# Hybrid attention, pooling and SwiGLU block on eight cores: last stores awaited behind the join, a hinted exit, a later table load and other vector durations in the planner

## What is computed

```python
u = rms_norm(h, norm_mix)
q, k, v, z, g_att, g_pool = split(u @ w_in)
att = dilated_attention(partial_rope(q), partial_rope(k), v)
pooled = einsum(multiscale_pool(z), w_pool_group) * pool_scale
merged = sigmoid(g_att) * (att @ w_att_branch) + sigmoid(g_pool) * (pooled @ w_pool_branch)
h = h + merged @ w_out
f = rms_norm(h, norm_ffn)
h = h + (silu(f @ w_gate) * (f @ w_up)) @ w_down
return rms_norm(h, norm_final)
```

## Time and profile before

| what | us |
|---|---|
| median of 3 runs (lowest to highest) | 1156.18 (1154.26 to 1157.77) |
| profiled execution, its own time | 1156.19 |
| its span (slowest core, core 1) | 1154.6 |
| TensorE busy in the span | 1117.1 |
| VectorE busy | 523.6 |
| ScalarE busy | 449.0 |

### The profile page before, as it was taken

One profiled execution on the slowest core, in us unless ns is written; L12 is line 12 of the kernel. 1 busy time (PEld: TensorE's weight loads), 2 busy tenths in 40 slices (PEclk: granted clock), 3 DMA queues, 4 the chain that ended last, 5 costly groups with the idle time before them and its releaser, 6 DMA issues.

```text
span 1154.6 us, 21542 instructions; the slowest of 8 cores (1139.4 to 1154.6 us)
## 1 busy us (share of the span) xinstructions
PE 1117.1 (97%) x8417; PEld 648.7 (56%) x8417; DVE 523.6 (45%) x786; ACT 449.0 (39%) x712; POOL 69.0 (6%) x134
## 2 busy tenths in 40 slices
PE   6999999998999999999999999999999999999995
PEld 4666667866685757544444444444444444444485
DVE  3565565356256426975334484212223343323244
ACT  4874655665466446742222132111121132231121
POOL 4120000000000000002000000000000000000000
PEclk7999999999999999999999999999999999999998
DMA  8986344334341455066620415533345255641412
GB/s 202 341 227 172 87 78 98 74 71 90 64 99 39 98 95 142 3 152 112 157 28 1 82 29 117 92 75 73 74 74 98 53 92 115 133 91 54 101 72 72
DMA packets 41068, 113.37 MB, mean 98 GB/s; under 512 B 4672, under 2 KB 10944, under 8 KB 36992
## 3 DMA queue, kind: packets, MB, share of 16 engines
q0 software_dynamic: 18656, 69.48, 30.9%
q1 hardware_dynamic: 21008, 40.92, 12.5%
q10 hardware_dynamic: 1296, 1.51, 0.4%
HBM read 145.80 MB, written 19.56 MB: 143 GB/s over the span
## 4 chain that ended last, share of the span: by engine, by line
PE 89%; DMA 3%; DVE 3%; ACT 2%; issue 1%; SPq 0%; POOL 0%; POOLq 0%; DVEq 0%; ACTq 0%
PE ps_all L433 89%; DVE arena L447 3%; ACT arena L438 2%; DMA arena<-xs 1%; DMA sa_1<-arena 1%; DMA sb_1<-arena 1%; DMA arena<-sb_1 0%; SPq L310 0%; DMA arena<-sa_1 0%; DVE arena L452 0%; POOL arena L310 0%; POOLq L336 0%; DVEq L322 0%; ACTq L322 0%; DVE arena L485 0%
## 5 line engine op out<-in xcount | busy, mean ns | idle before, releaser
L433 PE MATMUL ps_all<-arena 128*128 128x128 bf16 (+7 forms) x8417 | 1117.1, 297 | 26.5 <-ACT arena L438 14.9
L433 PEld LDWEIGHTS ps_all<-arena 128*128 128x128 bf16 (+1 forms) x8417 | 648.7, 105 | 494.7 <-issue 43.9
L438 ACT ACTIVATE arena<-ps_all 128x512 bf16<-128x512 f32 (+8 forms) x491 | 309.4, 660 | 497.3 <-PE ps_all L433 496.2
L447 DVE TENSOR_TENSOR arena<-arena 128x1024 bf16<-128x1024 bf16 (+11 forms) x308 | 224.6, 745 | 157.1 <-ACT arena L438 134.9
L447 DVE TENSOR_TENSOR arena<-ps_all,arena 128x496 bf16<-128x496 f32 (+4 forms) x160 | 114.9, 727 | 295.6 <-PE ps_all L433 281.8
L438 ACT ACTIVATE arena<-arena 128x512 f32<-128x512 f32 (+8 forms) x187 | 114.9, 632 | 126.4 <-DVE arena L447 104.7
L452 DVE SCALAR_TENSOR_TENSOR arena<-arena 128x512 bf16<-128x512 f32 (+6 forms) x172 | 99.4, 634 | 45.9 <-ACT arena L438 44.7
L452 DVE SCALAR_TENSOR_TENSOR arena<-arena,ps_all 128x496 f32<-128x496 f32 (+1 forms) x64 | 42.0, 666 | 75.7 <-PE ps_all L433 75.2
L438 ACT ACT_TABLE_LOAD x14 | 18.0, 1283 | 45.2 <-PE ps_all L433 39.8
L310 POOL DMA_DIRECT2D arena<-wq x36 | 19.2, 544 | 250.6 <-PE ps_all L433 248.0
L310 POOL DMA_DIRECT2D arena<-wgu x22 | 11.6, 530 | 300.6 <-PE ps_all L433 242.5
(11 more groups left out here) (8 smaller groups left out, 5.5 us busy)
## 6 DMA issues: line engine op xcount, KB each, us to landing
arena<-wgu POOLq DMA_DIRECT2D x22, 1024.0 KB, 8.2
arena<-xT POOLq DMA_DIRECT2D x24, 512.0 KB, 19.4
arena<-wd POOLq DMA_DIRECT2D x8, 1408.0 KB, 10.5
arena<-wq POOLq DMA_DIRECT2D x36, 256.0 KB, 5.9
arena<-wb POOLq DMA_DIRECT2D x24, 256.0 KB, 4.7
arena<-xT SPq DMA_DIRECT2D x8, 768.0 KB, 7.4
oT<-arena SPq DMA_DIRECT2D x24, 248.0 KB, 2.1
arena<-xs POOLq DMA_DIRECT2D x6, 512.0 KB, 20.1
```

What stands on the lines that cost most here:

```text
L433: return P.op("pe", lambda e: e.matmul(out, lhsT=lhsT, rhs=rhs, start=start, stop=stop, **kw), [lhsT, rhs], [out], (busy, 0.17))
L438: return P.op("act", lambda e: e.activation(out=out, in_=in_, func=func, **kw), rd, [out], (width(in_) / 1200 + 0.11, 0.08))
L447: return P.op("dve", lambda e: e.tensor_tensor(out=out, in0=in0, in1=in1, op=op), [in0, in1], [out], cost_dve(out, in0, in1))
```

## The change

Six edits. SyncE's wait for the last eight stores is taken out of the two programs: these stores count on a semaphore of their own, `fin`, and SyncE waits for it in the common end. The wait for all other stores is split into one ahead of the last eight outputs and one behind them. The jump from Second to the end gets a prefetch hint, 24 operations ahead of it on each engine. ScalarE's dummy activation moves from the common code behind the branch. In the last piece two tasks are popped per group of matmuls and not four. The planner's cost of a VectorE instruction that writes `arena` with a step other than one is multiplied, in its part that grows with n, by 2.2 for bf16 and 1.75 for f32.

```diff
+        self.fin = other.fin if other else es.enter_context(nc.semaphore("fin"))
+        self.last = 0
...
+    def dma_last(self, q, out, in_):
+
+        waits = self._waits(q, self._deps(q, [in_], [], True))
+        self.last += 16
+        self.ops[q].append((waits, lambda e: e.dma_start(out=out, in_=in_), (self.fin, 16)))
...
                 with eng.bass.body(second, valid_engines=[eng.engine]):
-                    progs[1].body(eng, progs[1].ops[e][n:])
-                    eng.br(end)
+                    k = max(n, len(progs[1].ops[e]) - 24)
+                    progs[1].body(eng, progs[1].ops[e][n:k])
+                    to_end = eng.mark_branch_hint_location()
+                    progs[1].body(eng, progs[1].ops[e][k:])
+                    eng.br(end).branch_hint(to_end)
                 with eng.bass.body(first, valid_engines=[eng.engine]):
                     progs[0].body(eng, progs[0].ops[e][n:])
                     eng.br(end)
                 eng.bass.switch_bb(end)
+                if e == "sp":
+                    assert progs[0].last == progs[1].last
+                    eng.wait_ge(progs[0].fin, progs[0].last)
...
     def cost_dve(*aps):
         n = width(aps[0])
         fast = all(ap.dtype == BF16 and ap.tensor.name == "arena" for ap in aps)
-        return (n / (1920 if fast else 960) + 0.14, 0.03)
+        apart = aps[0].tensor.name == "arena" and aps[0].ap[-1][0] != 1
+        return (n / (1920 if fast else 960) * ((2.2 if aps[0].dtype == BF16 else 1.75) if apart else 1) + 0.14, 0.03)
...
+    P.mark = {"act": len(P.ops["act"])}
     memset(onev, 1.0)
     act(f32(NW - 1, 1), onev[:, 0:1], AF.Square)
...
-    P.mark = {e: len(P.ops[e]) for e in P.ENGS}
+    P.mark = {e: P.mark.get(e, len(P.ops[e])) for e in P.ENGS}
...
-    def emit_out(slots, queues=("sp",)):
+    def emit_out(slots, queues=("sp",), last=False):
...
-            P.outs.append(P.dma(queues[C["o"] % len(queues)], T["oT"][c * 128:(c + 1) * 128, cols], o, more=True))
+            q, to = queues[C["o"] % len(queues)], T["oT"][c * 128:(c + 1) * 128, cols]
+            if last:
+                P.dma_last(q, to, o)
+            else:
+                P.outs.append(P.dma(q, to, o, more=True))
...
-            pop(tasks, 4)
+            pop(tasks, 2 if k == len(parts) - 1 else 4)
...
-        fin = eo if left > 1 else emit_out(halves[1 - left], ("sp", "act"))
+        fin = eo if left > 1 else emit_out(halves[1 - left], ("sp", "act"), left == 0)
...
+    P.wait("sp", P.outs[:-8])
     pop(tasks, 99)
-    P.wait("sp", P.outs)
+    P.wait("sp", P.outs[-8:])
```

## The result

The kernel after takes 1140.26 us in the median of 4 runs (1139.87 to 1141.96), the kernel before beside it 1156.97 us (4 runs, 1154.26 to 1162.02). The ratio is 0.9853, with a 95% interval of 0.9818 to 0.9889: 16.7 us less by the medians, 12.8 to 21 us by the interval. The forecast was 6.6 us less, and its range began at 1145.0 us: right in sign, too small by more than half.

A forecast was written before the change was run, and what follows sets the result against it. The prediction took TensorE on the odd cores, which run Second, as the bound nearly everywhere. From 1156.2 us it took 2.6 for the end and 4 for the scheduler, giving 1149.6 us; range 1145.0 to 1157.5 us.

The forecast's parts named there:

- Durations in the scheduler: Turns between pairs of heads: truer VectorE prices let the planner regain idle TensorE time, -4 us (from -10.8 to +10.5).
- second turn's chain: Turn at 364 to 418 us: VectorE, then the rope's round trips through memory, which no order of matmuls shortens.
- rival C: Both turns: a 5.3 us division block goes ahead of the rope on VectorE, +10.5 us, 1164.1 us in all; chance 0.12.
- Halving: TensorE's waits for VectorE and ScalarE, 255 to 480 us: half of 8.9 us regained, rounded to 4 us.
- The sign of being right that was set: TensorE's waits from 255 to 480 us fall below 6 us, with the strided VectorE instructions as long as before.
- left only the adds as news: Planner prices under the skill's striding rule: divisions stay at 0.69 us, adds' 12.8 of 33 us count; term about -1.5 us.
- Waits past the join: Kernel's end: SyncE jumps before waiting for the last stores, so the landing hides its jump; -2.6 us, bounds 0 and -2.6.
- Exit hint: Jump to the common end: already hidden under the last stores, so prefetching its code gives 0.
- The cover is the landing of 3.9 us: Kernel's end: the last stores' landing hides SyncE's jump; with a 2.3 us landing the hint gives at most 0.9 us.
- Pop, split wait and table load: Last piece and start: slower output tasks, SyncE's divided wait and ScalarE's single table load each give 0.
- B: Only the kernel's end gains; the new order moves TensorE's idle time without shrinking it; 1153.6 us, chance 0.25.
- D: Kernel's end: the hint displaces TensorE's own code before its last matmuls, +3.9 us, 1157.5 us in all; chance 0.08.

The follow-up runs named there:

- the square: Four kernels by hint and place of SyncE's wait; last matmul to end: ahead of join 11.3 or 11.8 us unhinted, 8.5 hinted; behind it 9.8 and 7.9.

## Why the prediction was wrong, point by point

**Durations in the scheduler: -4 forecast, -11.5 measured.** This is the step that failed: "Between, I take half of the 8.9 us, rounded to 4, since the turn at 260 us has filler enough and the second one is chained". Two things in it were wrong.

- The second turn's chain was read as fixed ("the chain passes through DMAs that no order of matmuls shortens"). No order of matmuls shortens it, but the plan also orders VectorE, and the chain began there, with the rope behind four divisions. The forecast had this mechanism in its hands as rival C, with the sign turned: a block of divisions of 5.3 us ahead of the rope was the state before, as the earlier trace rows (rope arithmetic at 377.33 us) and the timeline around it show, and the change took it away. Forcing the order alone gave 6.3 us, turning it back (and the rope further than before) cost 19.
- Halving had no row behind it. The waits in the earlier trace rows fell from 10.8 to 2.0 us, by 8.8 us: all of the 8.9 us that the forecast halved. Those ahead of 255 us fell a little too: over 40 to 490 us from 13.5 to 4.2, 9.3 us. On core 1 the clock adds some: its mean in 418 to 475 us rose from 0.97 in the earlier trace rows to 1.00, worth 0.03 x 57 = 1.7 us. These two are 11.0 of core 1's 13.5 us. Holes too short for the list of waits are not the rest: all of TensorE's idle time from 40 to 490 us fell from 14.2 to 4.7 us, by 9.5. What is left lies in what the profile counts as busy TensorE, and these rows do not split it.

The reason "dearer divisions become ready later" was named against C and was the clue, but the wrong price was watched: divisions become ready later by dearer adds, not by their own price. The sign of being right that was set, less than 6 us of waits in the window of the earlier trace rows, came (2.0 us), and it could not tell 4 us from 9. The Trainium skill (SBUF — State Buffer, Door 1: The DMA port swizzle), weighed there, left only the adds as news and made the term about -1.5 us. The trace still speaks against its rule for the divisions (1326 ns strided against 692), yet the adds' price alone brought 8.5 us and the divisions' price alone cost 2.2 us (by all the runs' odd cores 6.1 and 4.6 us): the term does not go by the us of price that a plan is short of.

**Waits past the join: -2.6 forecast.** The mechanism was right: SyncE's jump stands ahead of the landing and the 2.6 us ahead of its DRAIN are gone. Alone it gave 2.0 us (11.8 to 9.8), as SyncE's jump without a hint still ended up to 1.3 us behind the landing.

**Exit hint: 0 forecast, wrong.** The step "The cover is the landing of 3.9 us" failed twice without the hint: SyncE's jump came later than reckoned, as its issues took up to 1.93 us and not 0.33, so that the jump outlasted the landing by 0.4 to 1.3 us; and the landing itself came 1.3 us later than with the hint (medians of the odd cores). Together that is the 1.9 us of the square, twice the 0.9 us that the forecast gave as the most. Code fetched beside the stores is the likely reason, not a shown one. With both edits the end is 3.4 us shorter than before, 0.8 more than the term.

**Pop, split wait and table load: 0.** Right for the pop and the table load, within what these runs tell; the split of SyncE's wait was not tried by itself.

**Rivals.** B (the end alone) is out by the experiment with the prices alone; C is out as a forecast, though its mechanism was the cause, reversed; D (the hint harms) is out, as TensorE's jump fell to 452 ns and the last matmul was not late.

What stays open: the 5 us between the forced order and the true prices were split on core 1 only and not tried apart; and why stores were issued slowly in some of the kernels without the hint and not in others is not known.

## What to carry to other kernels

When a static scheduler gets truer durations, look for the queue whose order it will turn, not only for the idle time that it will fill: ask which long block stands ahead of the first step of the longest chain, on every engine that the plan orders. To see which price turns the order, ask whose result the competing block reads: here the price of the adds moved the divisions. Correct the prices together, since one half of the correction gained here and the other half alone lost. At the end of a program count an unhinted jump not only as time of the engine that jumps: here the last stores landed 1.3 us later without the hint.

## What the hardware showed that was not expected

Packets of code lie among those of the last stores. The view of the DMA queues counts them with the packets of the core's 16 DMA engines. In the kernel before, a packet of 16 KB of queue q8 and two of 8 KB of q14 lie between the last stores (1148 to 1150 us). In the kernel after, the last packet of q8 comes ahead of the stores (1131 to 1132.5 us), while four of q14 still lie beside them (1133 to 1138.5 us). The rows give packets, MB and share of 16 engines, for these three stretches:

```profile
q1 hardware_dynamic: 258, 0.22, 35.8%
...
q8 instruction: 1, 0.02, 5.2%
q14 instruction: 2, 0.02, 2.9%
```

```profile
q8 instruction: 1, 0.02, 5.6%
```

```profile
...
q1 hardware_dynamic: 576, 0.49, 27.4%
q14 instruction: 4, 0.03, 2.5%
```

The last landing of the odd cores came 8.1 to 8.5 us behind the last matmul before, and 7.5 to 7.9 us after. That the packet of q8 between the stores is what delays them is inferred from its place and from the kernels with and without the hint; it was not tried apart from the jump. The slow issues of up to 1.93 us need more than that packet, as the kernel before has the packet and not the slow issues.

Holes in TensorE's work went with a lower clock, but not each time. Where a kernel left holes of 1.9 to 2.7 us in this phase (order turned back, or the bf16 price alone), the granted clock of the same or the next stretch fell to 0.92 to 0.96 on most odd cores. With the bf16 price alone all four odd cores have the same hole in 300 to 345 us, and their clocks there are 0.92, 1.00, 0.92 and 0.96. With the order turned back the clock made 8.5 of 22 us on core 1, and 3.0 of 18 us on core 5.
